# Full-height second score matmuls in a two-branch attention block (one core)

## The reference, cut to what matters

```
s1 = einsum('bqhd,bkhd->bhqk', qb1, k1) * scale + bias      # contraction over 64
s2 = einsum('bqhd,bkhd->bhqk', qb2, k2) * scale + bias      # contraction over 64
p  = softmax(s1) - lam * softmax(s2)
```

```
s = einsum(q_nope, k_nope) + einsum(q_rope, k_rope)         # contractions over 128 and 64
```

## Time and profile before

| | |
|---|---|
| median of 3 runs | 1525.99 us (1525.85 to 1526.4) |
| span of the profiled execution, first to last instruction | 1524.1 us |
| TensorE busy with matmuls | 1504.3 us, 99% |
| VectorE busy | 766.2 us, 50% |
| ScalarE busy | 518.9 us, 34% |
| mean granted TensorE clock | 0.998 |

### The profile page before, as it was taken

The page is one execution under the profiler, slowest core; times in us unless marked ns, Lnnn a source line. Parts: engine busy times, 40 slices in busy tenths (PEclk is TensorE's granted clock), DMA queues, the critical chain, the costliest instruction groups (busy, mean ns, idle before and its releaser), DMA issues.

```text
span 1524.1 us, 19429 instructions
## 1 busy us (share of the span) xinstructions
PE 1504.3 (99%) x6996; PEld 1231.5 (81%) x6996; DVE 766.2 (50%) x1157; ACT 518.9 (34%) x781; POOL 34.1 (2%) x56
## 2 busy tenths in 40 slices
PE   6999999999999999999999999999999999999997
PEld 5788788788788887887788888888888888888886
DVE  6666566666655547676778322222223222253431
ACT  6334434334433334433345222222222222242321
POOL 0000000000000000000000000000000000000000
PEclk9999999999999999999999999999999999999999
DMA  6322222222223332222212333333333333344432
GB/s 200 89 70 83 69 83 73 79 80 71 76 76 83 85 95 76 63 69 61 61 57 69 86 97 98 97 98 94 98 96 96 99 97 94 102 150 153 152 102 111
DMA packets 236277, 140.46 MB, mean 92 GB/s; under 512 B 18640, under 2 KB 223568, under 8 KB 235728
## 3 DMA queue, kind: packets, MB, share of 16 engines
q1 hardware_dynamic: 236240, 139.97, 31.6%
HBM read 135.74 MB, written 4.19 MB: 92 GB/s over the span
## 4 chain that ended last, share of the span: by engine, by line
PE 98%; issue 1%; DVE 0%; ACT 0%; DMA 0%; POOL 0%; POOLq 0%; DVEq 0%; ACTq 0%
PE bank L1235 30%; PE bank L1236 29%; PE bank L1237 29%; PE bank L1289 2%; PE bank L1264 1%; PE bank L1266 1%; PE bank L1285 1%; PE bank L1280 1%; PE bank L1320 1%; PE bank L1314 1%; PE bank L1281 0%; PE bank L1282 0%; PE bank L1284 0%; DMA x_tok<-in_x_dram 0%; PE bank L1342 0%
## 5 line engine op out<-in xcount | busy, mean ns | idle before, releaser
L764 DVE TENSOR_TENSOR w_lo<-w_raw,w_hi 128x1024 fp32r<-128x1024 f32 (+1 forms) x238 | 288.3, 1211 | 534.0 <-ACT w_hi L445 533.1
L1235 PE MATMUL bank<-h_hi,w_hi 128*128 128x512 f32 x1296 | 512.4, 395 | 0.4 <-DVE k_hl L769 0.3
L1236 PE MATMUL bank<-h_lo,w_hi 128*128 128x512 f32 x1296 | 505.0, 390 | 0.0
L1237 PE MATMUL bank<-h_hi,w_lo 128*128 128x512 f32 x1296 | 504.8, 390 | 0.0
L445 ACT ACTIVATE w_hi<-w_raw 128x1024 fp32r<-128x1024 f32 (+1 forms) x238 | 250.0, 1050 | 567.4 <-DMA w_raw<-in_w_in_dram 339.0
L1235 PEld LDWEIGHTS bank<-h_hi,w_hi 128*128 128x128 f32 x1296 | 243.4, 188 | 55.2 <-issue 6.1
L1237 PEld LDWEIGHTS bank<-h_hi,w_lo 128*128 128x128 f32 x1296 | 243.3, 188 | 51.7
L1236 PEld LDWEIGHTS bank<-h_lo,w_hi 128*128 128x128 f32 x1296 | 243.6, 188 | 47.2
L465 ACT ACTIVATE e<-e,small 128x512 f32<-128x512 f32 x64 | 45.8, 716 | 139.4 <-DVE small L795 139.4
L1236 PE MATMUL bank<-w_lo,mg_hi 128*128 128x512 f32 x224 | 87.1, 389 | 0.0
L1237 PE MATMUL bank<-w_hi,mg_lo 128*128 128x512 f32 x224 | 87.1, 389 | 0.0
(11 more groups left out here) (173 smaller groups left out, 1622.7 us busy)
## 6 DMA issues: line engine op xcount, KB each, us to landing
w_raw<-in_w_in_dram SPq DMA_DIRECT2D x324, 256.0 KB, 3.1
w_raw<-in_w_out_dram SPq DMA_DIRECT2D x56, 256.0 KB, 2.8
w_raw<-in_w_oa_dram SPq DMA_DIRECT2D x32, 256.0 KB, 2.9
w_raw<-in_w_ob_dram SPq DMA_DIRECT2D x32, 256.0 KB, 3.0
x_tok<-in_x_dram SPq DMA_DIRECT2D x7, 1024.0 KB, 7.4
w_raw<-in_w_ukv_dram SPq DMA_DIRECT2D x16, 256.0 KB, 2.8
e_raw<-in_w_out_dram SPq DMA_DIRECT2D x8, 256.0 KB, 3.6
out_dram<-x_tok SPq DMA_DIRECT2D x8, 256.0 KB, 2.6
```

The source lines that it names most:

```text
L764: dve.tensor_tensor(w_lo[:, piece.slot, 0:cols], w_raw[:, piece.slot, 0:cols], w_hi[:, piece.slot, 0:cols].bitcast(F32), ALU.subtract).the ...
L1235: pe.matmul(dst, lhs_hi, rhs_hi, start=start, stop=False)
L1236: pe.matmul(dst, lhs_hi, rhs_lo, start=False, stop=False)
L1237: return pe.matmul(dst, lhs_lo, rhs_hi, start=False, stop=stop)
```

## The change: what it does

`ka_lo` gets a second plane (2 KB more per partition, over a place that is written again only later). Plane m holds k_lo of map m in its own half, and zeros in the other half, which POOL writes once at the start; TensorE waits for that beside `ones_set`. The two second matmuls of a branch A site then run over 128 rows: q_hi·k_lo + q_lo·0. In branch B the second rotary matmul runs over all 128 rows of `qr_hl` and `kr_lo`: q_hi·k_lo + q_lo·k_lo, a term more than before. No instruction changes its place, and none is removed; two memsets and a wait are added.

```diff
-        ka_lo = at("ka_lo", 198, [P, SEQ], F32R)
+        ka_lo = at("ka_lo", 198, [P, 2, SEQ], F32R)
...
+            pool.memset(ka_lo[HIGH, 0, :].bitcast(F32), 0.0).then_inc(zeros_set, 1)
+            pool.wait_ge(zeros_set, 1)
+            pool.memset(ka_lo[LOW, 1, :].bitcast(F32), 0.0).then_inc(zeros_set, 1)
+            pool.wait_ge(zeros_set, 2)
...
-                        last = dve.tensor_tensor(ka_lo[own, :], ACC[1][own, :], ka[own, m, :].bitcast(F32),
+                        last = dve.tensor_tensor(ka_lo[own, m, :], ACC[1][own, :], ka[own, m, :].bitcast(F32),
                                                  ALU.subtract)
...
                 for m, dst in enumerate((a, b)):
 
                     pe.matmul(dst[:, :], qa[:, m, q], ka[:, m, :], start=True, stop=False)
-                for m, (dst, own) in enumerate(((a, LOW), (b, HIGH))):
-                    last = pe.matmul(dst[:, :], qa[own, m, q], ka_lo[own, :], start=False, stop=True)
+                for m, dst in enumerate((a, b)):
+
+                    last = pe.matmul(dst[:, :], qa[:, m, q], ka_lo[:, m, :], start=False, stop=True)
...
                 pe.matmul(dst, qr_hl[:, q], kr_hi[:, :], start=False, stop=False)
-                pe.matmul(dst, qr_hl[own, q], kr_lo[own, :], start=False, stop=True).then_inc(scored, 1)
+                pe.matmul(dst, qr_hl[:, q], kr_lo[:, :], start=False, stop=True).then_inc(scored, 1)
...
             pe.wait_ge(ones_set, 3)
+            pe.wait_ge(zeros_set, 2)
```

More of the change, by code:

```diff
@@ L211, in hybrid_encoder @@
         ones_set = sem("ones_set")
+        zeros_set = sem("zeros_set")
         v_chain = sem("v_chain")
@@ L1264, in scores_a, with scores_b @@
                     pe.matmul(dst[:, :], qa[:, m, q], ka[:, m, :], start=True, stop=False)
-                for m, (dst, own) in enumerate(((a, LOW), (b, HIGH))):
-                    last = pe.matmul(dst[:, :], qa[own, m, q], ka_lo[own, :], start=False, stop=True)
+                for m, dst in enumerate((a, b)):
+                    last = pe.matmul(dst[:, :], qa[:, m, q], ka_lo[:, m, :], start=False, stop=True)
                 last.then_inc(scored, 1)
-            def scores_b(h, t, own, prev):
+            def scores_b(h, t, prev):
                 H = h + BH
@@ L1422, in b_extras @@
                 if s == 2 and cur:
-                    scores_b(h, 0, pair[1], prev)
-                    scores_b(h, 1, pair[1], prev)
+                    scores_b(h, 0, prev)
+                    scores_b(h, 1, prev)
                     pe.wait_ge(acc_read, h * 4 + (HEADS * 4 + 13))
@@ L1431, in b_extras @@
                 if s == 3 and cur:
-                    scores_b(h, 2, pair[1], prev)
-                    scores_b(h, 3, pair[1], prev)
+                    scores_b(h, 2, prev)
+                    scores_b(h, 3, prev)
                     turn_p_b(H, 0)
```

## The result

| | before | changed |
|---|---|---|
| median, us | 1526.08 (1525.85 to 1526.4, 4 runs) | 1507.95 (1507.93 to 1508.31, 4 runs) |
| span of the profiled execution, us | 1524.1 | 1506.1 |
| mean granted TensorE clock | 0.998 | 0.999 |

The ratio is 0.9882, with a 95% interval of 0.9868 to 0.9896: 18.1 us, 1.2%, faster. The forecast was 1508.4 with a range of 1506.0 to 1512.5.

A forecast was written before the change was run, and what follows sets the result against it. The prediction took TensorE's matmul starts to bound the kernel; 5.7 us from branch A plus 6.4 and 5.5 from branch B, 17.6 off 1525.99, gave 1508.4 us, with a stated range of 1506.0 to 1512.5.

The forecast's parts named there:

- What bounds the kernel: Whole kernel: TensorE, never fed too late, sets the time by the distance between matmul starts, 0.2265 us each when undisturbed.
- Part (1): Branch A, 32 sites: five distances take 1.13 us in place of 1.31, a gain of 0.18 each, 5.7 us.
- Part (2): Branch B, 32 sites: 0.40 us gained at 16 followed by score sites, 0.34 at 16 followed by transposes; 6.4 + 5.5 us.
- Part (3): Two added POOL memsets at the start: 0.2 to 1.3 us for both, hidden behind the wait for x; cost 0.
- Parts (4) and (5): DVE's subtractions into `ka_lo` cost 0; no new wait for TensorE, taken as 0 with up to 3 us kept for the range.
- R1: Pauses belong to the operand turn or bank write and stay, while branch A's overlap goes: slower, 1533.2 us; chance 0.03.
- R2: In branch B a wait for k_lo or the gate chain takes back most of 11.9 us: about 1517; chance 0.05.
- R3: Low-part matmuls still go out in pieces, or the full-height product runs at another pace: near 1526 us; chance 0.02.

The follow-up runs named there:

- a_full: The changed kernel with branch B's second rotary matmul put back to 64 rows, so only branch A is full-height; 1520.02 us, ratio 0.9961.
- same_half: The kernel before, with both 64-row matmuls of each branch A site in the lower half of the array; 1533.36 us, ratio 1.0047.
- b_full: The kernel before with only branch B's second rotary matmul made full-height, branch A keeping its 64-row pairs; 1513.93 us, ratio 0.9921.

## Why the prediction was right

**What bounds the kernel** held: TensorE's matmul starts set the time, and what they gave up in the two branches came off the end. The merge stage took the same 538.00 us.

**Part (1), branch A, 5.7 us**: 6.0 measured in a_full. One of its two terms was measured apart: the overlap is worth 7.3 us (same_half, 7.2 estimated; 7.20 over the stretch of branch A shown below, 439.71 us for 432.51). The pauses that went are what is left, 6.0 + 7.3 = 13.3 us (32 × 0.40 = 12.8 estimated).

The Trainium skill ("TensorEngine Tiling (Array Packing)", "Key Properties") states that different tiles work in parallel and that a change of the tiling mode drains TensorE. The traces agree with both: the starts of a pair are 3 ns apart and putting the two in one half cost 7.3 us, and the loads of the 64-row operands stood still for 11.5 and 11.4 us. What decided was the price of the turn against that of the overlap, and both came from rows of the kernel before.

**Part (2), branch B, 6.4 + 5.5 = 11.9 us**: 12.1 measured in b_full.

**Part (3), the memsets, 0**: 0.52 us each, inside the bounds of 0.2 to 1.3 for both, ended at 2.04 us, and nothing waited for them.

**Parts (4) and (5), no new wait**: branch B's idle TensorE time is 0.32 us in 252 after 0.27 in 262. The tightest wait kept its 0.80 us, for the reason given: no changed matmul lies between the start of that chain and the matmul that waits.

**The sum** was 17.6 and the measured difference 18.1. Part (1) came out 0.3 short and part (2) 0.2, and the traces show where. Branch A from its first score matmul to the first other than a projection in the next stage, before and after:

```profile
51.72 0.61 PE L1264 MATMUL bank<-ka,qa 128*128 128x512 f32 x2
...
484.23 0.61 PE L1314 MATMUL bank<-small,vT 128*128 128x1 f32 x5
```
```profile
51.85 0.61 PE L1270 MATMUL bank<-ka,qa 128*128 128x512 f32 x2
...
478.35 0.50 PE L1321 MATMUL bank<-small,vT 128*128 128x1 f32 x4
```

That is 432.51 us and then 426.50 (426.494 before rounding), 6.01 less; a_full takes 426.49 and b_full 432.51. The five distances per site were priced rightly but end too early: the four behind them took 0.93 us before at head 1, t = 1 (114.56 to 115.49) and take 0.91 now (113.56 to 114.47). Around branch B, from the same column spread ahead of it (565.10, now 559.22) to the same matmul of the merge stage (882.42, now 864.45), it took 317.32 us and takes 305.23, 12.09 less. There the 16 sites with transposes gain 0.35 each and not 0.34. The 0.13 us by which branch A starts later (51.85 against 51.72) lies within the scatter of that start, 51.56 to 52.11 in the eight profiled executions.

The stated range holds the measured time, but its own terms, added up, give 1506.3 to 1513.5 and not 1506.5 to 1512.5.

**The rivals.** R1 (the pauses stay and the overlap goes, 1533.2) fell with b_full, where only the height of one matmul changed and 12.1 us went. Its price for the overlap was right all the same: same_half lost just that. R2 (a wait in B takes the time back) and R3 did not come: B kept all of its gain.

## What to carry to other kernels

A matmul over half the rows is not cheaper than a full one when its neighbours are full-height: it takes its distance and another 0.35 to 0.43 us for the turn there and back. If zeros or a harmless extra term can fill the other rows, fill them. Halves pay once enough of them stand together, in different halves, for one turn: here one pair per turn lost 0.19 us (6.0 over 32 sites), and two pairs won 0.02. This was run for 64 rows and 512 columns only, in a kernel that TensorE bounds. To price it before a run, add up the distances between matmul starts from the last full-height one until they are back at the undisturbed 0.2265, in branch A the sixth matmul behind the site and not the second, since the recorded durations (498 against 390 ns) don't tell it; and look at the idle time ahead of the loads, which shows the turn.

## What the runs showed that I had not expected

The loads of two halves lie on top of each other as well. In the kernel before the 64 loads of branch A's pairs, 183 ns each, are busy for 6.0 us, half of their sum of 11.7. In same_half they are busy for 9.4 us, with the same 11.5 us of idle ahead of them; even in one half they overlap in part:

```profile
L1266 PEld LDWEIGHTS bank<-ka_lo,qa 64*128 64x128 f32 x64 | 9.4, 184 | 11.5 <-issue 11.5
```

And the second of two 64-row matmuls in one half costs no more than a full-height one: 0.66 − 0.43 = 0.23 us. A lone one only looks slow (0.43 us to the next start), because the turn back stands behind it.
